# Chunked mLSTM in a fused decoder step: the chunk states move ahead of the last page sum on VectorE, and the first head runs two projection tiles further

## The chip, the cores and the metric

The kernel runs on one core of a Trainium2 chip as one program. The metric is the device time of one execution in microseconds (us). The engines named below are TensorE (PE in the profile, its weight loads PEld), VectorE (DVE), ScalarE (ACT), GpSimd (POOL) and SyncE (SP), whose queue issues most of the transfers.

## The reference

One layer of a hybrid decoder over a prompt of 512 tokens and 8 single sample tokens, all in fp32:

```python
mod = silu(c) @ w_ada + b_ada            # shift, scale, gate
h   = rms_norm(x, norm_g) * (1 + scale) + shift
z   = h @ w_in                           # att q,k,v,gate | mLSTM q,k | v | o | gate | i,f | ga | gm
ya  = (moba_attention(q, k, v) * silu(za)) @ w_att
# mLSTM: 4 heads, key width 128, value width 256
qk  = silu(causal_conv4(qk_pre));  m = running max;  w = exp(decays - m)
num = a * (C @ q) + (q @ k.T * w) @ v;   den = a * (n @ q) + rowsum(q @ k.T * w)
h_m = num / max(|den|, exp(-m));  C, n = decayed C, n plus k.T @ v
ym  = (rms_norm(h_m) * m_norm_g * sigmoid(o) * silu(zm)) @ w_mlstm
y   = rms_norm(x + gate * ((sigmoid(ga) * ya + sigmoid(gm) * ym) @ w_out))
```

For the 8 sample tokens attention reads whole pages of a cache (`cache_v`, 128 pages of 128 rows by 512 values), weighted with a softmax over the blocks that each query chose ("the page choice").

## The kernel before, in words

The program is written engine by engine, each with its own instruction list, and the lists meet in counting semaphores. Nothing is ordered by a scheduler: the order of the lines is the order of the work on each engine.

**Projection tiles.** The long product h @ w_in is cut into tiles of 128 output columns, numbered n (`T_ML` is the first of the mLSTM, 8 for each head). A tile takes 48 matmuls of 260 columns (`ztile`, L565): fp32 is split into a high and a low part, and three products are summed. Ahead of it SP loads the weights into one of four slots of `wraw` (L390), ACT rounds them to the high part (`high`, L1025), POOL subtracts to get the low part (`low`, L1521); both go into one of two slots. Behind it ACT copies the result out of PSUM (`leave`, L1030). Tile n needs tile n-2 to have left, and `high` of tile n needs tile n-2 to be done.

**One head of the mLSTM.** Tiles 0 and 1 of a head are q and k before the convolution, 2 and 3 are v, 4 and 5 the output gate, 6 and 7 the silu gate. After tiles 0 and 1 DVE convolves (`convolve`, L1911 and L1914), ACT applies silu (L1302) and computes the decays `wt` and `qd`. PE multiplies q and k (L787), turns k (L792) and v (L807) over; DVE forms `wt`, `qd` and `kw` (L2037, L2039, L2042), the weights' products. PE forms each chunk's state from `kw` (L823, "k_mm"), DVE runs them together into `Cs` (L2050, L2052) and raises `cs_rdy`; PE needs it for the outputs (L829, L831, "pv"). ACT squares these (L1321), DVE normalises (`norm`, from L2007), ACT scales (L1327), PE turns them over (L844), DVE applies the gates (L2066, L2069). PE lays tiles 4 to 7 of the head between those steps, and tiles 0 and 1 of the next head follow.

**Page values beside it.** Under each head the pages of `cache_v` are worked off in 8 steps of 4 pages: SP loads a step into one of four slots (L407), POOL multiplies it by its weights (`value_step`, L1599), and DVE sums two steps at a time (`value_pair`, L1993 and L1998). A pair's sum frees its two slots (`pair_free`), and SP waits for that before it loads the next steps; weights' tiles stand behind those loads in the same queue. PE sums over the partitions at the end of the head's last tile (`page_sums`, L580). The last pair of head h-1, `value_pair(6, h-1)`, stands in head h on DVE, between `kw` and the chunk states.

**The first head** is written apart: during it the page choice for the samples is finished on DVE (`choice_sums` L1976, `choice_total` L1980, `choice_normalise`), with a product on PE in between (L813) that waits for the sums and stands ahead of k_mm.

Of the kernel before, what the change touches and what calls it, by code (L numbers as in the profile page):

```python
# [20 lines left out]
ACT = mybir.ActivationFunctionType  # L21
# [17 lines left out]
MH, MQ, MV = 4, 128, 256  # L39
# [50 lines left out]
def decoder_step(nc, I, O):  # L90
# [14 lines left out]
    with ExitStack() as ctx:  # L105
# [443 lines left out]
        def _(pe):  # L549
# [223 lines left out]
            def mlstm(h, first, begun=False):  # L773
                n = T_ML + 8 * h
                if not first:
                    if not begun:
                        ztile(0, n, hH, hL)
                    ztile(1, n + 1, hH, hL)
                    spread_max(h)
                    ztile(2, n + 2, hH, hL)  # L780
                    ztile(3, n + 3, hH, hL)
                    pe.wait_ge(hn_ev, 2 * h + 1)
# [26 lines left out]
                if first:  # L809

                    pe.wait_ge(vt_ev, 1)
                    pe.wait_ge(sel_dve, 7)
                    mm(ps[:, 7, 256:320], ones[:, :], mxA[:, :], start=True, stop=True).then_inc(sel_pe, 1)  # L813
                else:
                    ztile(0, n + 4, hH, hL)
# [8 lines left out]
                last.then_inc(k_mm, 1)  # L824
                if not first:
                    ztile(1, n + 5, hH, hL)
# [5 lines left out]
                last.then_inc(pv_mm, 1)  # L832
                if not first:
                    ztile(2, n + 6, hH, hL)
                ztile(3, n + 7, hH, hL, pages_of=None if first else h)
                if first:
                    ztile(0, n + 8, hH, hL)
                pe.wait_ge(hn_ev, 2 * h + 3)
# [176 lines left out]
        def _(act):  # L1015
# [269 lines left out]

            def mlstm(h, first):
                n, quad = T_ML + 8 * h, T_ML // 4 + 2 * h
                if first:
                    decays(h, True)
                else:  # L1290
                    high(2, n + 2, quad)
                    act.wait_ge(z_done, n + 3)
                    last_tap(0, h)
                    leave(0, n, pre[:, 0, 3:3 + NT], ACT.Copy, chunk(preS, h))
                    high(3, n + 3, quad)
                    act.wait_ge(z_done, n + 1 + 3)
                    last_tap(1, h)
                    leave(1, n + 1, pre[:, 1, 3:3 + NT], ACT.Copy, chunk(preS, h + MH))
                    decays(h, False)
                    for e in range(2):  # L1300
                        act.wait_ge(cv_rdy, 2 * h + e + 1)
                        f(qkc[:, e, :], ps[:, 4 + e, :], ACT.Silu).then_inc(sg_rdy, 1)  # L1302
                    high(0, n + 4, quad + 1)
                    leave(0, n + 2, mvT[:, 0, :], ACT.Copy, chunk(vS, 2 * h))
                    high(1, n + 5, quad + 1)
                    leave(1, n + 3, mvT[:, 1, :], ACT.Copy, chunk(vS, 2 * h + 1))
# [4 lines left out]
                if first:  # L1311
                    high(0, n + 8, quad + 2)
                    leave(0, n + 6, gz[:, 0, :], ACT.Silu, chunk(gzS, 2 * h))
                else:
                    for u in range(2):
                        high(2 + u, n + 6 + u, quad + 1)
                        leave(u, n + 4 + u, go[:, u, :], ACT.Sigmoid, chunk(goS, 2 * h + u))
# [11 lines left out]
                if not first:  # L1329
                    high(0, n + 8, quad + 2)  # L1330
                    leave(0, n + 6, gz[:, 0, :], ACT.Silu, chunk(gzS, 2 * h))
                high(1, n + 9, quad + 2)
                if first:
                    leave(1, n + 7, gz[:, 1, :], ACT.Silu, chunk(gzS, 2 * h + 1))
                else:
                    act.wait_ge(z_done, n + 10)
# [12 lines left out]
            mlstm(0, True)  # L1349
            with act.Fori(0, MH - 1) as h:  # L1350
                mlstm(h + 1, False)
            act.dma_start(O["conv_s"][0, :, 0:2, :], I["state_conv"][0, :, 1:3, :]).then_inc(st_misc, 16)
# [154 lines left out]
        def _(pool):  # L1507
# [98 lines left out]
            for j in range(3):  # L1606
                low(j, T_ML + 4 + j)
            pool.wait_ge(w_exp, 1)
            low(3, T_ML + 7)
            causal_weights(0)  # L1610
            pool.wait_ge(sel_act, 2)
            value_step(0, 0)
            low(0, T_ML + 8)
            for s in range(1, 4):
                value_step(s, 0)
            low(1, T_ML + 9)
            low(2, T_ML + 10)
            value_step(4, 0)
            low(3, T_ML + 11)
            value_step(5, 0)  # L1620
# [73 lines left out]
        def _(dve):  # L1694
# [333 lines left out]
            def mlstm(h, first):  # L2028
# [4 lines left out]
                if not first:  # L2033
                    value_pair(4, h - 1, h == 1)
                dve.wait_ge(st_mm, h + 1)
                dve.wait_ge(w_rdy, h + 1)
# [7 lines left out]
                if first:  # L2044
                    choice_sums()
                    choice_total()
                else:
                    value_pair(6, h - 1, h == 1)
                dve.wait_ge(k_mm, h + 1)
# [7 lines left out]
                if first:  # L2057
                    choice_normalise()
                norm(h)
                value_pair(0, h, first)  # L2060
# [235 lines left out]
```

## Time and profile before

| what | us |
|---|---|
| median of 3 runs | 740.52 (737.6 to 742.81) |
| the profiled execution | 742.74 |
| its span, first to last instruction | 741.0 |
| PE busy in the span | 664.1 (90%) |
| POOL, DVE, ACT busy | 434.9, 482.4, 333.2 |
| mean granted clock of TensorE | 0.949 of full speed |

The busy times are sums over all stages. The mLSTM heads lie between about 262 and 500 us of the span: the first from 262 to 305, then three of about the same shape. Times in the rows below are us from the span's start. A matmul's own duration includes its latency, so consecutive starts tell more than durations do.

### The profile page before, as it was taken

What the parts mean: (1) busy time and instruction counts of PE and PEld (TensorE: products, weight loads), DVE (VectorE), ACT (ScalarE), POOL (GpSimd) and SP (SyncE); (2) the same over time, 40 slices, a digit from 0 to 9 for tenths busy, and PEclk for the clock granted to TensorE, in tenths of its full rate; (3) what the DMA queues carried; (4) which work ended last, traced back from release to release, by engine and by line L of the source; (5) the groups of instructions that cost most, each with busy time, mean ns of one, the idle gap of its engine ahead of it and who ended that gap; (6) DMA issues with size and microseconds to landing.
All of it is one profiled execution on the core that took longest, in us unless ns stands there. A gap on an engine that the chain in (4) does not pass through costs nothing.

```text
span 741.0 us, 14542 instructions
## 1 busy us (share of the span) xinstructions
PE 664.1 (90%) x4898; PEld 600.4 (81%) x4898; DVE 482.4 (65%) x500; ACT 333.2 (45%) x732; POOL 434.9 (59%) x290
## 2 busy tenths in 40 slices
PE   2899898797997977987999799799999999999996
PEld 0578787586877866976999699699799999999974
DVE  0627587798989953995587579565564549444435
ACT  5645838164571451642554336253322224332643
POOL 5212586474965337488589498944386567666520
PEclk9899999899999896998999899899899999999998
DMA  8968379898896883477568756756946446832302
GB/s 315 343 212 251 115 214 268 242 270 266 268 297 192 284 239 103 111 219 205 157 211 240 209 168 183 210 150 192 274 117 193 124 144 181 264 96 85 87 23 93
DMA packets 156908, 144.79 MB, mean 195 GB/s; under 512 B 7547, under 2 KB 115152, under 8 KB 156852
## 3 DMA queue, kind: packets, MB, share of 16 engines
q1 hardware_dynamic: 142984, 137.15, 62.2%
q10 hardware_dynamic: 13876, 7.02, 3.1%
q8 instruction: 27, 0.44, 0.2%
q14 instruction: 21, 0.17, 0.1%
HBM read 135.10 MB, written 9.11 MB: 195 GB/s over the span
## 4 chain that ended last, share of the span: by engine, by line
PE 37%; issue 19%; POOL 19%; DVE 10%; SPq 7%; DMA 4%; ACT 4%; POOLq 0%; ACTq 0%; DVEq 0%
PE ps L565 27%; POOL sb_wL L1521 8%; POOL sb_arenaA L1599 7%; POOL sb_arenaA L1567 4%; PE ps L995 3%; SPq L406 2%; DVE sb_arenaA L1998 2%; SPq L407 2%; DMA sb_arenaA<-in_w_ada 2%; DMA sb_wraw<-in_w_in 2%; PE ps L597 1%; DVE sb_arenaB L1998 1%; PE ps L829 1%; DVE sb_arenaA L1993 1%; PE ps L936 1%
## 5 line engine op out<-in xcount | busy, mean ns | idle before, releaser
L1521 POOL TENSOR_TENSOR sb_wL<-sb_wraw,sb_wH 128x512 fp32r<-128x512 f32 (+1 forms) x168 | 217.0, 1308 | 202.6 <-ACT sb_wH L1025 188.7
L565 PE MATMUL ps<-sb_hH,sb_wH 128*128 128x260 f32 x1152 | 242.6, 292 | 4.2 <-POOL sb_wL L1521 4.2
L565 PE MATMUL ps<-sb_hH,sb_wL 128*128 128x260 f32 x1152 | 235.9, 287 | 0.0
L565 PE MATMUL ps<-sb_hL,sb_wH 128*128 128x260 f32 x1152 | 235.8, 287 | 0.0
L565 PEld LDWEIGHTS ps<-sb_hH,sb_wH 128*128 128x128 f32 x1152 | 182.5, 193 | 18.7 <-issue 13.0
L565 PEld LDWEIGHTS ps<-sb_hL,sb_wH 128*128 128x128 f32 x1152 | 181.7, 193 | 0.0
L565 PEld LDWEIGHTS ps<-sb_hH,sb_wL 128*128 128x128 f32 x1152 | 181.7, 193 | 0.0
L1025 ACT ACTIVATE sb_wH<-sb_wraw 128x512 fp32r<-128x512 f32 (+1 forms) x168 | 98.9, 612 | 179.4 <-PE ps L565 125.7
L1599 POOL TENSOR_TENSOR sb_arenaA<-sb_arenaA 128x2048 f32<-128x2048 f32 x28 | 101.4, 3624 | 2.5 <-DMA sb_arenaA<-in_cache_v 2.5
L1567 POOL TENSOR_TENSOR sb_arenaA<-sb_arenaA 128x1024 f32<-128x1024 f32 x22 | 63.5, 2906 | 40.9 <-DMA sb_arenaA<-in_cache_k 40.9
L1852 DVE TENSOR_REDUCE sb_arenaA<-sb_arenaA 128x2048 f32 (+1 forms) x32 | 73.0, 2285 | 5.7 <-POOL sb_arenaA L1567 3.3
L1848 DVE TENSOR_TENSOR sb_arenaA<-sb_arenaA 128x2048 f32<-128x2048 f32 x21 | 54.5, 2594 | 9.4 <-DMA sb_arenaA<-in_cache_k 8.4
L1993 DVE TENSOR_REDUCE sb_arenaA<-sb_arenaA 128x512 f32<-128x4096 f32 x7 | 53.4, 7634 | 0.0
L1998 DVE TENSOR_REDUCE sb_arenaA<-sb_arenaA 128x512 f32<-128x4608 f32 x4 | 34.3, 8587 | 4.8 <-POOL sb_arenaA L1599 4.8
L1030 ACT ACTIVATE sb_arenaB<-ps 128x520 f32<-128x520 f32 (+1 forms) x57 | 33.9, 595 | 0.9 <-ACT sb_kqN L1241 0.8
L1998 DVE TENSOR_REDUCE sb_arenaB<-sb_arenaA 128x512 f32<-128x4608 f32 x3 | 25.3, 8418 | 13.8 <-POOL sb_arenaA L1599 13.8
L829 PE MATMUL ps<-sb_arenaB 128*128 128x257 f32 x32 | 16.8, 655 | 18.1 <-DVE sb_arenaB L2052 18.1
L671 PE MATMUL ps<-sb_arenaB 64*128 64x384 f32 (+3 forms) x64 | 20.9, 462 | 8.1 <-ACT sb_arenaA L1170 6.7
L829 PEld LDWEIGHTS ps<-sb_arenaB 128*128 128x128 f32 x32 | 10.0, 329 | 21.7 <-DVE sb_arenaB L2052 19.5
L1145 ACT ACTIVATE sb_arenaB<-ps,sb_nmx 128x512 f32<-128x512 f32 (+3 forms) x32 | 16.4, 526 | 22.9 <-DVE sb_nmx L1834 22.8
L1321 ACT ACTIVATE sb_arenaB<-ps 128x256 f32<-128x256 f32 x16 | 5.9, 384 | 46.0 <-PE ps L831 46.0
L597 PE MATMUL ps<-sb_arenaA,sb_gated 128*32 128x512 f32 x112 | 16.1, 691 | 10.6 <-DMA sb_arenaA<-in_w_ada 10.6
(406 smaller groups left out, 941.8 us busy)
## 6 DMA issues: line engine op xcount, KB each, us to landing
sb_wraw<-in_w_in SPq DMA_DIRECT2D x64, 512.0 KB, 5.4
sb_arenaA<-in_cache_k SPq DMA_DIRECT2D x128, 256.0 KB, 3.2
sb_arenaA<-in_cache_v SPq DMA_DIRECT2D x128, 256.0 KB, 3.2
sb_arenaA<-in_w_ada SPq DMA_DIRECT2D x6, 2048.0 KB, 12.1
sb_arenaB<-in_state_C SPq DMA_DIRECT2D x8, 512.0 KB, 4.2
sb_wraw<-in_w_mlstm SPq DMA_DIRECT2D x8, 512.0 KB, 4.5
sb_wraw<-in_w_out SPq DMA_DIRECT2D x8, 512.0 KB, 3.8
sb_arenaB<-in_x_prompt SPq DMA_DIRECT2D x1, 2048.0 KB
```

The costliest lines, as they stand in the source:

```text
L565: last = mm(ps[:, 2 * s + a, 0:HALF], w[:, s, k, :], x[:, k, a * HALF:(a + 1) * HALF], start=(k == 0 and w is wH and x is xH), stop=(k == ...
L597: last = mm(ps[32 * g:32 * g + 32, bank, :], (hS if i == W_Q else cT)[:, k, :], ada[:, i % 2, k, :], start=(k < 4), stop=(k >= 4))
L829: last = mm(ps[:, 4 + q, 0:MV + 1], wt[:, q, :], v1[:, q, :], start=True, stop=(q == 0))
L1025: f(wH[:, j % 2, part], wraw[:, j % 4, part], ACT.Copy).then_inc(hi_done, 1)
L1030: ins = f(halves(dst), zps(j % 2), func)
L1521: tt(wL[:, j % 2, part], wraw[:, j % 4, part], wH[:, j % 2, part].bitcast(F32), ALU.subtract)\
L1567: last = tt(two, two, qbc[:, s // 4:s // 4 + 1, :].broadcast_to([P, 2, AW]), ALU.mult)
L1599: tt(heads, heads, score[:, bass.ds((8 * h + s) * 32, 32)].unsqueeze(2).broadcast_to([P, 32, DH]), ALU.mult).then_inc(pool_mult, 1)
L1848: chain(tt(four, four, qbc[:, s // 4:s // 4 + 1, :].broadcast_to([P, STEP_PAGES, AW]), ALU.mult))
L1852: v.tensor_reduce(score[:, bass.ds((8 * t + s) * 32, 32)], page[:, s % 4, :].rearrange("p (g n) -> p g n", n=DH), AX, ALU.add)\
L1993: v.tensor_reduce(vhalf, vpairs[0], AX, ALU.add).then_inc(pair_free[0], 1)
L1998: v.tensor_reduce(vacc[e], vpairs[1], AX, ALU.add).then_inc(pair_free[1], 1)
```

## The change

Four engines' lists are edited; no arithmetic changes.

- DVE: for all heads but the first, `value_pair(6, h-1)` moves from ahead of the chunk states to behind them (ahead of `norm`). In the first head `choice_sums` moves from behind `kw` to ahead of `wt`.
- PE: in the first head tile 7 moves from behind pv to ahead of k_mm, tile 0 of the next head from there to between k_mm and pv, and tile 1 of the next head, so far the second head's, stands behind pv. The second head begins with `spread_max`.
- ACT: the high parts and the copies out follow that order, and the high part of the next head's tile 2 is made there too.
- POOL: in the first head the low part of tile 7 goes ahead of the wait for the decays and of the causal mask (L1593), and value steps and low parts alternate.

```diff
@@ PE, mlstm
                 if not first:
                     if not begun:
                         ztile(0, n, hH, hL)
-                    ztile(1, n + 1, hH, hL)
+                        ztile(1, n + 1, hH, hL)
                     spread_max(h)
@@
                     mm(ps[:, 7, 256:320], ones[:, :], mxA[:, :], start=True, stop=True).then_inc(sel_pe, 1)
+                    ztile(3, n + 7, hH, hL)
                 else:
                     ztile(0, n + 4, hH, hL)
@@
                 last.then_inc(k_mm, 1)
-                if not first:
+                if first:
+                    ztile(0, n + 8, hH, hL)
+                else:
                     ztile(1, n + 5, hH, hL)
@@
                 last.then_inc(pv_mm, 1)
-                if not first:
+                if first:
+                    ztile(1, n + 9, hH, hL)
+                else:
                     ztile(2, n + 6, hH, hL)
-                ztile(3, n + 7, hH, hL, pages_of=None if first else h)
-                if first:
-                    ztile(0, n + 8, hH, hL)
+                    ztile(3, n + 7, hH, hL, pages_of=h)
@@ ACT, mlstm
-            def mlstm(h, first):
+            def mlstm(h, first, begun=False):
...
-                    high(2, n + 2, quad)
+                    if not begun:
+                        high(2, n + 2, quad)
...
                     high(0, n + 8, quad + 2)
                     leave(0, n + 6, gz[:, 0, :], ACT.Silu, chunk(gzS, 2 * h))
+                    high(1, n + 9, quad + 2)
+                    leave(1, n + 7, gz[:, 1, :], ACT.Silu, chunk(gzS, 2 * h + 1))
+                    high(2, n + 10, quad + 2)
...
-                high(1, n + 9, quad + 2)
-                if first:
-                    leave(1, n + 7, gz[:, 1, :], ACT.Silu, chunk(gzS, 2 * h + 1))
-                else:
+                    high(1, n + 9, quad + 2)
...
             mlstm(0, True)
-            with act.Fori(0, MH - 1) as h:
-                mlstm(h + 1, False)
+            mlstm(1, False, True)
+            with act.Fori(0, MH - 2) as h:
+                mlstm(h + 2, False)
@@ POOL
+            low(3, T_ML + 7)
             pool.wait_ge(w_exp, 1)
-            low(3, T_ML + 7)
             causal_weights(0)
             pool.wait_ge(sel_act, 2)
-            value_step(0, 0)
-            low(0, T_ML + 8)
-            for s in range(1, 4):
+            for s in range(4):
                 value_step(s, 0)
-            low(1, T_ML + 9)
-            low(2, T_ML + 10)
+                low(s, T_ML + 8 + s)
             value_step(4, 0)
-            low(3, T_ML + 11)
             value_step(5, 0)
@@ DVE, mlstm
                     value_pair(4, h - 1, h == 1)
+                if first:
+                    choice_sums()
                 dve.wait_ge(st_mm, h + 1)
...
                 if first:
-                    choice_sums()
                     choice_total()
-                else:
-                    value_pair(6, h - 1, h == 1)
                 dve.wait_ge(k_mm, h + 1)
...
                 if first:
                     choice_normalise()
+                else:
+                    value_pair(6, h - 1, h == 1)
                 norm(h)
```

## Rows read from the trace of the kernel before

**Rows 1.** The waits, PE: who waited for whom, us in total, times, longest.

```profile
PE ps L829 <- DVE sb_arenaB L2052: 18.1, 4, 5.6
```

**Rows 2.** Timeline of PE, third head, last row fourth: start, us, what, count [idle before <- releaser].

```profile
394.83 0.49 PE L565 MATMUL ps<-sb_hH,sb_wH 128*128 128x260 f32 x2
...
400.66 1.90 PE L823 MATMUL ps<-sb_arenaB 128*128 128x257 f32 x8
...
413.56 2.08 PE L829 MATMUL ps<-sb_arenaB 128*128 128x257 f32 x4 [5.25 <-DVE sb_arenaB L2052]
...
419.22 0.59 PE L565 MATMUL ps<-sb_hH,sb_wH 128*128 128x260 f32 x2
...
478.57 2.08 PE L829 MATMUL ps<-sb_arenaB 128*128 128x257 f32 x4 [5.25 <-DVE sb_arenaB L2052]
```

**Rows 3.** Timeline of DVE, third head.

```profile
398.07 0.68 DVE L2042 SCALAR_TENSOR_TENSOR sb_arenaB<-ps,sb_wa 128x512 f32<-128x512 f32 x1
402.92 8.47 DVE L1998 TENSOR_REDUCE sb_arenaB<-sb_arenaA 128x512 f32<-128x4608 f32 x1 [4.18 <-POOL sb_arenaA L1599]
411.53 0.43 DVE L2050 COPY sb_arenaB<-ps 128x257 f32<-128x257 f32 x1
411.99 1.51 DVE L2052 SCALAR_TENSOR_TENSOR sb_arenaB<-sb_arenaB,sb_wa,ps 128x257 f32<-128x257 f32 x3
421.21 0.16 DVE L2007 TENSOR_SCALAR sb_dl<-ps 128x4 f32<-128x4 f32 x1 [7.70 <-ACT sb_arenaB L1321]
...
438.40 8.62 DVE L1998 TENSOR_REDUCE sb_arenaA<-sb_arenaA 128x512 f32<-128x4608 f32 x1 [1.61 <-POOL sb_arenaA L1599]
```

**Rows 4.** Windows: us, busy of PE, PEld, DVE, ACT, POOL, granted clock, DMA.

```profile
402.30:408.30 6.00, 6.00 (x50) 5.79 (x48) 5.38 (x1) 1.80 (x4) 6.00 (x4) 1.00 0.89 279
...
413.50:419.30 5.80, 5.74 (x15) 4.60 (x15) 0.01 (x1) 0.00 (x0) 1.51 (x1) 0.52 0.79 235
```

**Rows 5.** Timeline of SP's queue, third head.

```profile
412.21 3.83 SPq L407 DMA_DIRECT2D sb_arenaA<-in_cache_v  x4
416.32 0.38 SPq L390 DMA_DIRECT2D sb_wraw<-in_w_in  x1
```

**Rows 6.** The page, DMA issues: count, KB each, us to landing.

```profile
sb_wraw<-in_w_in SPq DMA_DIRECT2D x64, 512.0 KB, 5.4
```

**Rows 7.** Windows: one period of the third head (same columns).

```profile
380.00:444.00 64.00, 58.76 (x448) 56.57 (x447) 46.21 (x33) 29.28 (x67) 48.70 (x26) 0.95 0.67 198
```

**Rows 8.** Timeline of PE, first head and the start of the second.

```profile
272.87 1.04 PE L807 MATMUL ps<-sb_ident,sb_arenaB 128*128 128x128 f32 x8
280.51 0.66 PE L813 MATMUL ps<-sb_mxA,sb_ones 128*128 128x64 f32 x2 [6.60 <-DVE sb_mxA L1976]
...
286.77 2.08 PE L829 MATMUL ps<-sb_arenaB 128*128 128x257 f32 x4 [2.07 <-DVE sb_arenaB L2052]
...
292.57 0.69 PE L565 MATMUL ps<-sb_hH,sb_wH 128*128 128x260 f32 x2
...
328.55 1.07 PE L807 MATMUL ps<-sb_ident,sb_arenaB 128*128 128x128 f32 x8 [2.76 <-ACT sb_vS L1032]
```

**Rows 9.** Timeline of DVE, first head to the second head's convolution.

```profile
274.57 3.29 DVE L2039 TENSOR_TENSOR sb_arenaB<-sb_arenaB 128x384 f32<-128x384 f32 x1
...
278.38 1.98 DVE L1976 TENSOR_REDUCE sb_mxA<-sb_arenaA 128x64 f32<-128x1024 f32 x1
...
294.74 0.16 DVE L2007 TENSOR_SCALAR sb_dl<-ps 128x4 f32<-128x4 f32 x1 [7.29 <-ACT sb_arenaB L1321]
...
305.83 1.42 DVE L2066 SCALAR_TENSOR_TENSOR ps<-ps,sb_vcol,sb_arenaB 128x512 f32<-128x512 f32 x2 [1.29 <-PE ps L844]
...
317.21 0.82 DVE L1911 TENSOR_SCALAR ps<-sb_arenaB,sb_vcol 128x512 f32<-128x512 f32 x1 [0.22 <-DVE sb_arenaA L1998]
```

**Rows 10.** Timeline of ACT: end of the page choice's weights, second head's last silu.

```profile
271.44 0.29 ACT L1268 ACTIVATE sb_selfp<-sb_selfp 128x64 f32<-128x64 f32 x1
...
323.53 0.60 ACT L1302 ACTIVATE sb_arenaB<-ps 128x512 f32<-128x512 f32 x1 [2.49 <-DVE ps L1914]
```

## The prediction

> **What bounds the kernel now.** I read the table of busy times first: PE is busy 664.1 of 741.0 us, more than any other engine, so what is to be had without taking work from PE is its idle time, and the time in which its clock is low. The waits of PE come next. They show the idle time as few, large pieces: 18.1 us in four waits of pv (L829) for the last instruction of the chunk states on VectorE (L2052), one in each head [rows 1], and 6.60 us in one wait of the page choice's product (L813) for `choice_sums` [rows 8]. Both lie where the change is made.
>
> The timeline of the third head tells what such a wait costs. The tile behind k_mm starts at about 402.2 and takes as long as the one ahead of it, 400.66 - 394.83 = 5.83 us; so PE is done with it near 408.1. pv starts only at 413.56, and lasts to 419.22, 5.66 us [rows 2]. In that stretch the granted clock is 0.52 of full speed, so the lower level of 1.2 GHz, where it was 1.00 (2.4 GHz) in the tile before the idle time [rows 4]. PE's idle time therefore costs twice: 5.25 us, and about half of the 5.66 us after it, 2.83 us. A second way gives the same: k_mm's four products take 402.2 - 400.66 = 1.56 us at full clock, 0.39 us each, so pv's seven would take 2.7 instead of 5.66, 2.9 us saved.
>
> Why is VectorE late? It has `kw` at 398.75 and k_mm is over at 402.2, but it first waits 4.18 us for GpSimd's last value step and then sums the pair, 402.92 to 411.4. The states take 411.53 to 413.5, 2.0 us [rows 3]. So 9 us of the queue stand between the states and their inputs, none of them needed by the states.
>
> **The third and fourth head.** The states now start at 402.3 and end at 404.3, while PE is in its tile until 408.1: the cover is 3.8 us. pv runs 408.1 to 410.9 at full clock. ScalarE's squares follow, and `norm` started 421.21 - 419.22 = 2.0 us behind pv's end [rows 2, 3]; that makes 412.9. VectorE's moved pair now runs from 404.4 (GpSimd's step was ready at 402.9) to 412.9 with its 8.47 us. The two meet, so the pair is just hidden; I allow 0.2 us for it. What follows hangs on pv and `norm`: scaling, the high and low part of the next head's tile 0, tiles 6 and 7. All moves up by 5.25 + 2.83 - 0.2 = 7.9 us.
>
> Does anything behind keep it from staying? I laid one period out again with PE's work back to back. Its length was 478.57 - 413.56 = 65.0 us, from one head's pv to the next's [rows 2], and becomes 57.1, which is PE's own work at full clock. GpSimd is busy 48.70 us in 64 and VectorE 46.21 [rows 7]; both fit in 57, each with some 8 us of slack. SyncE is the closest. The moved pair frees page slots 2 and 3 and ended 0.8 us before the page loads at 412.21; they took 3.83 us to issue, and the weights of the next head's tile 1 stood behind them, at 416.32 [rows 5]. Now the pair ends at 412.9, so these weights are issued near 417.8 and land 5.4 us later [rows 6], 423.2. PE comes to that tile at 431.6 (pv's end 410.9, two tiles 11.7, page sums and turning over some 2.9, one tile 5.8, in all 431.3), and both parts of it need about 4 us: a margin of 4 us. The page loads are later against PE by 1.5 + 8 us only for this one pair; GpSimd takes them when it has the low part of tile 0 done, some 0.6 us later than otherwise. The convolution starts when the pair of steps 2 and 3 is summed, and the start of that sum kept its distance to PE in my layout within 0.2 us. So each of these two heads gives 7.9 us.
>
> **The states beside GpSimd.** `L2052` now runs while GpSimd multiplies or subtracts. Its three instructions took 1.51 us at 411.99, when GpSimd was busy as well. `qd` (L2039), which reads two tensors of SBUF, took 3.29 us in the first head [rows 9], where a value step ran. Were each of the three states to take that in place of its 0.5 us, they would take 3 x 2.8 = 8.4 us more and end at 412.7, and PE would idle 4.6 us again. The Trainium skill (GPSIMD Engine Reference, the table of the engine's SBUF interfaces) says that GpSimd contends with VectorE instructions that have two SBUF inputs or run in a two-port mode. The states read one tensor from SBUF and one from PSUM, so by that rule they are free of it, and 1.51 us agrees; I take no cost.
>
> **The first head.** PE turned v over until 273.9, then idled 6.60 us and did the page choice's product at 280.51, k_mm, and pv from 286.77 to 292.57 with 2.07 us of idle time in between; pv's 5.8 us are again the slow ones [rows 8]. The weights that `choice_sums` needs are there at 271.7 [rows 10]. Moved ahead, it runs 271.8 to 273.8, the product follows at 274.1 or so, and tile 7 at 274.7. `wt`, `qd` and `kw` end near 278.4 even if `qd` takes its 3.29 us again, hidden by the tile, which ends at 280.6. Were that cover gone, PE would wait 3.7 us. k_mm to 282.2, tile 8 to 288.1 with the states under it (284.5), pv to 291.1, tile 9 to 297. The ends of the queues of ACT and POOL hold: the high parts of tiles 7, 8 and 9 are wanted 2 us or more after they can be made; ScalarE waits for tile 8's end at 288.1 to make half of tile 10, and is free when pv ends at 291.1.
>
> So pv ends 1.5 us earlier, and PE has tile 9 behind it, which it did not have before. But the second head's start is set by VectorE, not by PE: `norm` 294.74 becomes 293.2; the first pair's sum, the gates (whose 1.29 us of waiting for PE falls away, since the turning over comes after tile 9 at 298.3) and the second pair's sum follow back to back, and the convolution starts at 314.4 in place of 317.21 [rows 9]: 2.8 us. Its last silu was at 323.53 [rows 10] and comes at 320.8. PE, which has tiles 10 and 11 left, finishes them near 312.1 (about 1.5 us of it a new wait for ScalarE, which copies the state out and issues two stores before it empties tile 8). Then it idles until 321.4, **9.3 us**: the time that the earlier tiles won is held here, and is no gain by itself.
>
> Such an idle time lowers the clock. What was slow after 5.25 us of it was the next 5.7 us [rows 2, 4]. v's turning over waits here for its copy, as it did for 2.76 us before [rows 8], now until 325.8; behind it tile 12 runs, slow for its first half: 2.9 us. It ends near 335.4, where it ended 335.2 before: no gain by then. From there the second head is as the third: k_mm, a tile to 342.9, no wait for the states (VectorE has them at 339), pv to 345.8, where it was 354.2. The first two heads give **8.3 us**, with 11.2 if the clock is up by tile 12, and 5.5 if k_mm is slow as well.
>
> **The sum.** 8.3 + 2 x 7.9 = 24.1 us. The stage behind the heads starts from the fourth head's last pair of sums and page loads, which keep their distance; nothing there is changed. 742.74 - 24.1 = 718.6 for the profiled execution. That one is 2.2 us above the median of the three runs; from the median it is 716.4. I say 717.
>
> **Rivals.**
> *(a) The order's next limit bites.* The layout has VectorE, SyncE's page loads and GpSimd each with a few us to spare, and durations of transfers vary more than that when 8 us less are there for the same bytes (DMA share 0.67 in the period [rows 7], it would be 0.76). For it: the pair sum's end and `norm` meet exactly, and ScalarE's wait for weights. If each of three heads keeps 3 us of idle time and with it no full fall of the clock, the gain is 24.1 - 9 = 15 us: 727.5 from the profiled time, 725.5 from the median.
> *(b) The clock does not fall at the second head, and smaller waits close up:* 24.1 + 2.9 + 1 = 28: 712.5 from the median. Against it: 9.3 us are more than any idle time that left it up.
> *(c) It is the page loads' turn: slower.* The moved pair frees slots 2 and 3 later, and the weights stand behind those loads. Place: SyncE's queue at tile 9 of each head. It decides from the point where the pair ends more than 4 us later than my 412.9. It begins to cost more than the change brings at 12 us, which needs GpSimd's last step (ready at 402.9, VectorE at 404.4) some 13 us late. Then each of three heads would lose its 7.9 and 3 to 5 us more with a low clock behind: about +12 us, 752. Nothing in the profile points to it: that step never waited for its pages.
> *(d) The states' move does nothing,* because pv waits for something else too. pv waits for `cs_rdy` alone behind k_mm, and L2052 ends 0.1 us before pv starts [rows 2, 3]. If it were so, only the first head's 2 to 3 us would be left: 738.
>
> **Chances.** Forecast 62%, (a) 20%, (b) 10%, (c) 3%, (d) 5%. The forecast's own range is 713 to 721 (one head's 2.9 us of clock either way, and 1 us of the runs' spread). The range takes in (b)'s 712.5 and the nearer half of (a): 712 to 727. A measurement of this kernel tells a change of about 1%, 7.4 us, from none. Faster by over 1%: forecast, (a) and (b), with a little taken off: 0.91. Within 1%: 0.05. Slower: 0.04.
>
> **What would show it.** Right: the idle time in front of L829 gone in all heads, the granted clock 1.00 during pv, L2052 ahead of the L1998 that writes to arenaB, a period of 57 us, the idle time at L813 gone and a new one of about 9 us in front of the second head's L787, with a low clock after it. Wrong: idle time in front of a tile's first matmul, released by GpSimd's L1521, in heads 3 and 4 (then (a) or (c)), or `norm` starting over 1 us behind the squares; and a second head that starts earlier than 320, or later.

## The result, and the profile after

| | before | after |
|---|---|---|
| median of the runs, us | 739.06 (734.34 to 742.81) | 710.21 (707.32 to 720.91) |
| the profiled execution / its span | 742.74 / 741.0 | 707.32 / 705.6 |
| PE busy | 664.1 (90%) | 648.2 (92%) |
| mean granted clock | 0.949 | 0.974 |

The ratio is 0.960, with an interval of 0.952 to 0.968. One execution of the changed kernel, the one of 720.91 us, was in a slower state, and the ratio is formed without it. I had said 717, with 712 to 727 as the range; the time lies 1.8 us below the range. Two later measurements of the same kernel gave 0.972 and 0.964; the three are weighed below.

PE's busy time fell by 16 us though it runs the same 4898 matmuls: that is the clock, not the work (the mean granted clock rose from 0.949 to 0.974). The page and PE's waits after (who waited for whom, us in total, times, longest):

```profile
PE 648.2 (92%) x4898; PEld 588.7 (83%) x4898; DVE 485.6 (69%) x500; ACT 331.8 (47%) x731; POOL 434.5 (62%) x290
```

```profile
PE ps L597 <- DMA sb_arenaA<-in_w_ada: 10.4, 3, 8.2
PE ps L787 <- issue: 9.3, 1, 9.3
...
PE ps L565 <- POOL sb_wL L1526: 3.1, 1, 3.1
...
PE ps L807 <- ACT sb_vS L1035: 1.6, 2, 1.0
```

Pv's waits for the states, 18.1 us in [rows 1], are gone from the list, and so is the 6.6 us wait of the choice's product for VectorE. A new line stands there: L787, the second head's first product, 9.3 us. "Issue" means that the profile names no releaser. The code has three waits in front of it: for the first head's scaled outputs, for its gates, and for the silu behind the convolution. The first two were over long before (the gates' last instruction on VectorE ended at 302.1); the last silu on ScalarE ended at 317.56, and L787 starts at 317.66:

```profile
316.96 0.60 ACT L1306 ACTIVATE sb_arenaB<-ps 128x512 f32<-128x512 f32 x1 [2.50 <-DVE ps L1915]
```

PE's timeline after, second and third head, beside [rows 2, 8] (L824, L832 and L834 are the old L823, L829 and L831):

```profile
317.66 2.04 PE L787 MATMUL ps<-sb_arenaB 128*128 128x128 f32 x8 [9.27 <-issue]
319.50 1.06 PE L792 MATMUL ps<-sb_ident,sb_arenaB 128*128 128x128 f32 x4
321.58 1.06 PE L807 MATMUL ps<-sb_ident,sb_arenaB 128*128 128x128 f32 x8 [1.02 <-ACT sb_vS L1035]
322.40 0.49 PE L565 MATMUL ps<-sb_hH,sb_wH 128*128 128x260 f32 x2
...
335.70 1.03 PE L832 MATMUL ps<-sb_arenaB 128*128 128x257 f32 x4
...
338.55 0.59 PE L565 MATMUL ps<-sb_hH,sb_wH 128*128 128x260 f32 x2
...
393.05 1.03 PE L832 MATMUL ps<-sb_arenaB 128*128 128x257 f32 x4
...
449.81 1.03 PE L832 MATMUL ps<-sb_arenaB 128*128 128x257 f32 x4
```

Pv now follows its tile at once and takes 338.55 - 335.70 = 2.85 us in place of 5.66. From pv of the second head to pv of the fourth it is 449.81 - 335.70 = 114.1 us, two periods of 57.35 and 56.76 us.

VectorE's timeline after, second head, beside [rows 3]. The states come first, then the pair (L1999), then `norm`:

```profile
325.23 0.70 DVE L2045 SCALAR_TENSOR_TENSOR sb_arenaB<-ps,sb_wa 128x512 f32<-128x512 f32 x1
330.18 0.43 DVE L2050 COPY sb_arenaB<-ps 128x257 f32<-128x257 f32 x1 [4.24 <-PE ps L824]
330.64 1.52 DVE L2052 SCALAR_TENSOR_TENSOR sb_arenaB<-sb_arenaB,sb_wa,ps 128x257 f32<-128x257 f32 x3
332.08 8.50 DVE L1999 TENSOR_REDUCE sb_arenaB<-sb_arenaA 128x512 f32<-128x4608 f32 x1
340.73 0.16 DVE L2008 TENSOR_SCALAR sb_dl<-ps 128x4 f32<-128x4 f32 x1
```

Windows after (us, busy of PE, PEld, DVE, ACT, POOL, granted clock, DMA): the second head's first products, its tile 4 (tile 12 of the count), and one period of the later heads, beside [rows 4, 7]:

```profile
317.60:320.10 2.50, 2.44 (x11) 2.47 (x12) 2.50 (x1) 1.93 (x5) 1.94 (x2) 0.50 1.07 349
322.40:328.30 5.90, 5.90 (x52) 5.90 (x51) 3.54 (x4) 1.57 (x3) 5.90 (x4) 1.00 0.57 158
...
335.70:392.70 57.00, 56.45 (x454) 55.19 (x453) 46.88 (x33) 29.20 (x67) 50.17 (x26) 1.00 0.76 226
```

In the period PE is busy 56.45 of 57.0 us at a clock of 1.00; it bounds the later heads completely. GpSimd has 6.8 us left, VectorE 10. In the first head PE's idle time has shrunk to 0.25 us in front of the choice's product and 0.99 us in front of a later tile, and the second head's convolution starts at 310.65. VectorE's timeline there:

```profile
299.46 1.39 DVE L2068 SCALAR_TENSOR_TENSOR ps<-ps,sb_vcol,sb_arenaB 128x512 f32<-128x512 f32 x2
300.89 1.23 DVE L2071 TENSOR_TENSOR sb_gated<-ps,sb_arenaB 128x1024 f32<-128x1024 f32 x1
302.03 8.40 DVE L1999 TENSOR_REDUCE sb_arenaA<-sb_arenaA 128x512 f32<-128x4608 f32 x1
310.65 0.81 DVE L1912 TENSOR_SCALAR ps<-sb_arenaB,sb_vcol 128x512 f32<-128x512 f32 x1 [0.22 <-DVE sb_arenaA L1999]
```

**Where the 35.4 us of span went.** I laid both traces beside one another at five points on PE: an earlier product of the page choice, L799, in front of which nothing is changed, L787 of the second head, pv of the second head and of the fourth, and the samples' first product (L936, after L939). The last column is what my sum has for the same stretch; differences are taken before rounding.

| stretch | before | after | less | my sum |
|---|---|---|---|---|
| start to L799 (unchanged code) | 265.8 | 263.0 | 2.7 | 0 |
| to the second head's L787 | 58.5 | 54.6 | 3.8 | 2.8 |
| to its pv | 24.2 | 18.0 | 6.2 | 2.7 |
| to the fourth head's pv | 130.1 | 114.1 | 16.0 | 15.8 |
| to the samples' product | 53.0 | 49.4 | 3.6 | 2.8 |
| to the end (unchanged code) | 209.4 | 206.4 | 3.1 | 0 |

A stretch ends where pv starts, so the clock that pv itself gains counts in the line behind it: 2.8 us of each pv, the fourth's in the fifth line. So 29.6 us lie in the heads, where I had 24.1, and 5.8 us in stretches that the change doesn't touch. The largest difference from my sum, 3.5 us, stands in the third line, from the second head's L787 to its pv.

### The profile page after: what moved, and what is told of

The parts are those of the page before. It is cut to its first block, busy times and chain, and to the rows that moved or that the text cites. A ratio compares the mean times of both kernels' runs of the same rounds, so it can differ in the third digit from the quotient of the medians.

```text
span 705.6 us, 14507 instructions
## 1 busy us (share of the span) xinstructions
PE 648.2 (92%) x4898; PEld 588.7 (83%) x4898; DVE 485.6 (69%) x500; ACT 331.8 (47%) x731; POOL 434.5 (62%) x290
## 4 chain that ended last, share of the span: by engine, by line
PE 53%; DVE 14%; issue 10%; SPq 9%; ACT 5%; DMA 4%; POOL 4%; ACTq 0%; DVEq 0%; POOLq 0%
PE ps L565 39%; SPq L406 5%; SPq L407 4%; DVE sb_arenaA L1999 4%; PE ps L998 3%; DVE sb_arenaA L1849 2%; DMA sb_wraw<-in_w_in 2%; POOL sb_wL L1526 2%; POOL sb_arenaA L1604 1%; DVE sb_arenaB L1999 1%; DMA sb_arenaB<-in_x_sample 1%; DVE sb_arenaA L1853 1%; PE ps L824 1%; ACT sb_wH L1028 1%; DMA sb_arenaA<-in_cache_k 1%
## 5 line engine op out<-in xcount | busy, mean ns | idle before, releaser
L565 PEld LDWEIGHTS ps<-sb_hH,sb_wH 128*128 128x128 f32 x1152 | 180.6, 192 | 19.3 <-issue 12.5
L565 PEld LDWEIGHTS ps<-sb_hH,sb_wL 128*128 128x128 f32 x1152 | 179.7, 191 | 0.0
L1572 POOL TENSOR_TENSOR sb_arenaA<-sb_arenaA 128x1024 f32<-128x1024 f32 x22 | 61.2, 2807 | 37.3 <-DMA sb_arenaA<-in_cache_k 37.3
L1999 DVE TENSOR_REDUCE sb_arenaA<-sb_arenaA 128x512 f32<-128x4608 f32 x4 | 34.2, 8552 | 5.5 <-POOL sb_arenaA L1604 5.5
L2195 DVE TENSOR_TENSOR sb_arenaB<-ps,sb_arenaB 128x520 f32 x8 | 5.6, 700 | 30.1 <-PE ps L565 30.1
L1999 DVE TENSOR_REDUCE sb_arenaB<-sb_arenaA 128x512 f32<-128x4608 f32 x3 | 25.5, 8504 | 0.0
L597 PE MATMUL ps<-sb_arenaA,sb_gated 128*32 128x512 f32 x112 | 15.4, 671 | 10.7 <-DMA sb_arenaA<-in_w_ada 10.4
L2129 DVE CAST sb_kqr<-sb_rowsel 40x128 fp32r (+1 forms) x8 | 6.8, 855 | 20.3 <-PE ps L939 19.9
L671 PEld LDWEIGHTS ps<-sb_arenaB 64*128 64x128 f32 x64 | 10.0, 190 | 13.0 <-ACT sb_arenaA L1173 5.3
```

The lines of the kernel that those rows point to most:

```text
L565: last = mm(ps[:, 2 * s + a, 0:HALF], w[:, s, k, :], x[:, k, a * HALF:(a + 1) * HALF], start=(k == 0 and w is wH and x is xH), stop=(k == ...
L671: last = mm(ps[:, b, c:c + (q + 1) * P], qT[r, q * P:(q + 1) * P], kT[r, 0:(q + 1) * P], start=True, stop=True)
L1572: last = tt(two, two, qbc[:, s // 4:s // 4 + 1, :].broadcast_to([P, 2, AW]), ALU.mult)
L1999: v.tensor_reduce(vacc[e], vpairs[1], AX, ALU.add).then_inc(pair_free[1], 1)
```

## The experiments

**The two parts alone.** First the pair's move by itself, on the kernel before:

```diff
@@ DVE, mlstm, kernel before
-                else:
-                    value_pair(6, h - 1, h == 1)
                 dve.wait_ge(k_mm, h + 1)
...
                     choice_normalise()
+                else:
+                    value_pair(6, h - 1, h == 1)
```

> The kernel before with one edit: value_pair(6, h-1) behind the chunk states on VectorE. Theory 1 (a wait for the states costs its idle time and the slow clock after it): three waits of 5.3 to 5.6 us and 2.8 us of clock behind each go, 3 x 8 = 24 us less than before; the first head keeps its 6.6 and 2.1 us of idle time; period 57 us. Rival (the heads are only free because the first head runs ahead): the second head keeps a wait and the gain is 16 us or less.

715.12 us, ratio 0.972 (0.966 to 0.978), 23 us less. Pv to pv over two periods took 114.0 us. In its waits L829 is left with the first head's alone:

```profile
PE ps L813 <- DVE sb_mxA L1976: 6.6, 1, 6.6
...
PE ps L829 <- DVE sb_arenaB L2050: 2.1, 1, 2.1
```

So all three waits go without the first head's part, and the rival falls. Then the reverse, the changed kernel with the pair put back:

> The changed kernel with value_pair(6, h-1) put back ahead of the states. Theory 1: the second head's convolution starts some 3 to 4 us earlier than before and nothing else is won: 4 us less than before, with the idle time in front of L787 near 9 us and three waits of pv of 5 to 6 us. Together with the pair alone it makes the whole change's 29. Rival (the long idle time lowers the clock for a tile): 1 us less than before. Rival (the two parts need one another): both alone give much less than 29 in sum.

735.54 us, ratio 0.997 (0.993 to 1.001). Its waits:

```profile
PE ps L832 <- DVE sb_arenaB L2054: 14.6, 3, 5.3
...
PE ps L787 <- issue: 9.2, 1, 9.2
```

The three waits are back (4.2, 5.0 and 5.3 us), and the first head's part alone is worth 0.3%, 2.7 us where I expected 4, which is no more than the interval. Measured beside one another, the pair's move alone and the whole change took 715.12 and 715.36. Later both were measured again, with more executions:

> The kernel before with the pair's move alone, again, beside the whole change on the same chip. From the first page product of the choice to pv of the second head it took 77.3 us where the whole change took 72.7 and 75.1: so 2 to 4 us more than the whole change. If the first head's part is worth nothing, the two are equal within 1 us.

714.20, ratio 0.967 (0.964 to 0.971), against 711.55, 0.964 (0.961 to 0.968), for the whole change: 2.7 us more, but the intervals overlap.

**Which part of the first head's edit counts.** VectorE's two moves with the tiles, high and low parts where they were:

```diff
@@ DVE, mlstm, kernel before, with the pair's move as above
+                if first:
+                    choice_sums()
                 dve.wait_ge(st_mm, h + 1)
...
-                    choice_sums()
                     choice_total()
```

> The kernel before with VectorE's two moves alone (choice_sums ahead of wt, value_pair(6) behind the states); the tiles of the first head stand as before. Theory 1: the product for the choice no longer waits 6.6 us, k_mm starts 2 to 4 us earlier, and since the second head's start hangs on VectorE, which gains the same there as with the tiles moved, the stretch from the choice's product to the second head's pv takes 73 to 75 us as in the changed kernel: the tiles' new order is worth nothing by itself. Rival (the tiles' order matters): 76 to 77 us, as with the pair alone, and 2 us more in all than the changed kernel.

711.90, ratio 0.965 (0.962 to 0.969). From L799 to the second head's pv it took 337.55 - 263.64 = 73.9 us, where the changed kernel took 72.7, 75.1 and 74.3 in its three profiles, and the pair alone 77.3 and 76.3. PE's timeline in its first head:

```profile
275.12 0.43 PE L813 MATMUL ps<-sb_mxA,sb_ones 128*128 128x64 f32 x2 [0.25 <-ACT sb_arenaB L1309]
277.00 2.82 PE L823 MATMUL ps<-sb_arenaB 128*128 128x257 f32 x8 [1.45 <-DVE sb_arenaB L2044]
281.90 2.08 PE L829 MATMUL ps<-sb_arenaB 128*128 128x257 f32 x4 [2.07 <-DVE sb_arenaB L2051]
```

PE idles here in small pieces, and is there for the second head all the same: it waits 0.62 us in front of L787, where the changed kernel waits 9.27. The two numbers agree with the changed kernel's: the tiles' new order, which is most of the diff, is worth nothing that I can measure. It mostly moves PE's idle time from the first head to in front of L787.

**The changed kernel again.**

> The changed kernel again, for a second profile. If the clock behind the second head's idle time was up early by the way the kernel works, L787 to the next k_mm takes 10.6 us again and the span lies within 2 us of 705.6. If it is chance, tile 12 takes 5.8 us in some executions and up to 8.7 in others, and the span moves by up to 3 us at each such place. Against before: 29 us less.

715.36, ratio 0.972 (0.968 to 0.976); span 714.2. L787 to k_mm took 10.9 us, but L799 came at 266.8, 3.8 us later than in the first profile, in unchanged code. A third measurement:

> The changed kernel a third time, for what it is worth on average: its median was 29 us under the kernel before in one session and 23 us in the next. If my sum of 24 is right and the rest was chance, 22 to 28 us less than before, ratio 0.963 to 0.970. If the first session's 29 is the kernel's, 0.960 or less.

711.55, ratio 0.964 (0.961 to 0.968). The three ratios, 0.960, 0.972 and 0.964, make 29.6, 20.7 and 26.6 us of 740. And the kernel before:

> The kernel before, for a second profile. What lies in front of the first changed instruction took 263.0 us and 266.8 us in two profiles of the changed kernel, so it moves by 4 us by itself. Three waits of 5.3 us in front of L829 and a granted clock of 0.52 behind each again, if they follow from the order of the work.

733.77, a single execution; L799 at 262.0, waits of 5.28 and 5.27 us in front of pv in the third and fourth head, but 3.6 in the second, and 4.08 in front of the choice's product instead of 6.60. In the second head the clock was low in tile 12 this time (L787 to k_mm 13.1 us, against 11.0 in [rows 8]'s profile), and that hid 2 us of pv's wait: what the clock took from PE there, VectorE had been making PE wait for anyway.

From L799 to the samples' product the kernel before took 265.8 and 262.2 us in its two profiles, the changed one 236.2, 239.5 and 237.9. The means differ by **26.1 us**. That is my best number for the change, cleared of the unchanged parts; it rests on two and three profiles, which differ among themselves by up to 3.6 and 3.3 us.

**Where the pair may stand.** The changed kernel with the pair one step later:

```diff
@@ DVE, mlstm, changed kernel
                     choice_normalise()
-                else:
-                    value_pair(6, h - 1, h == 1)
                 norm(h)
+                if not first:
+                    value_pair(6, h - 1, h == 1)
```

> The changed kernel with value_pair(6, h-1) behind norm: the pair ends some 11 us later against PE, so its page slots, and the weights behind their loads in SyncE's queue, come 11 us later. By my prediction's margin of 4 us, PE waits for tile 1 of the next head, or for the page sums and the convolution, 4 to 6 us in each of three heads, and with some slow clock: 12 to 20 us more than the changed kernel, some 725 to 730. If the margin were over 11 us, nothing would change (710).

748.24, ratio 1.014 (1.008 to 1.020): 1.4% slower than the kernel before, and 32.9 us more than the changed one measured beside it, where I expected 12 to 20. Timelines of the second head's end, VectorE, SyncE's queue, GpSimd, ScalarE and PE:

```profile
346.67 8.52 DVE L1999 TENSOR_REDUCE sb_arenaB<-sb_arenaA 128x512 f32<-128x4608 f32 x1
```

```profile
356.01 3.83 SPq L407 DMA_DIRECT2D sb_arenaA<-in_cache_v  x4
360.12 0.38 SPq L390 DMA_DIRECT2D sb_wraw<-in_w_in  x1
```

```profile
363.21 3.62 POOL L1604 TENSOR_TENSOR sb_arenaA<-sb_arenaA 128x2048 f32<-128x2048 f32 x1 [11.71 <-DMA sb_arenaA<-in_cache_v]
366.79 2.52 POOL L1526 TENSOR_TENSOR sb_wL<-sb_wraw,sb_wH 128x512 fp32r<-128x512 f32 x2
```

```profile
364.50 1.15 ACT L1028 ACTIVATE sb_wH<-sb_wraw 128x512 fp32r<-128x512 f32 x2 [13.13 <-DMA sb_wraw<-in_w_in]
```

```profile
368.11 0.51 PE L565 MATMUL ps<-sb_hH,sb_wH 128*128 128x260 f32 x2 [3.85 <-POOL sb_wL L1526]
...
393.73 1.97 PE L807 MATMUL ps<-sb_ident,sb_arenaB 128*128 128x128 f32 x8 [3.41 <-ACT sb_vS L1035]
```

The pair ends at 355.2, 15.5 us behind pv's start at 339.7; in the changed kernel that distance is 4.9 (340.6 and 335.7). So it ends 10.6 us later against PE, as I expected. Its slots' pages are issued at 356.0, and GpSimd waits 11.7 us for them. The weights of the next head's tile 1 stand behind those loads, at 360.1, and ScalarE waits 13.1 us for them. The low part of that tile comes after both, and PE waits 3.85 us for it. Later weights are late too: in front of the third head's L807 PE waits 3.41 us (0.56 in the changed kernel), and over the kernel ScalarE's waits for weights grew from 41.0 to 94.3 us. This is the mechanism of my rival (c), at the place that I gave. The changed kernel escapes it because its pair ends in time. There the same low part starts at 352.24:

```profile
352.24 2.54 POOL L1526 TENSOR_TENSOR sb_wL<-sb_wraw,sb_wH 128x512 fp32r<-128x512 f32 x2
```

Half of it is done at 353.5, which is all that PE waited for above, and PE comes to this tile near 359.0. That is a reserve of some 5.5 us, an estimate from these rows, where the prediction had 4. No run has the pair between the two places, so where the loss begins isn't shown.

**The long idle time and the clock.** PE busy in it:

```diff
@@ PE, mlstm, changed kernel
                     pe.wait_ge(hn_ev, 2 * h + 1)
+                    if begun:
+                        for _ in range(36):
+                            mm(ps[:, 6, 0:P], ident[:, :], ident[:, :], start=True, stop=True)
```

> The changed kernel, with 36 products of the identity with itself (into an unused bank) in the second head's idle time of 9.3 us, so that PE is busy in it; their result is thrown away. Theory 2 (the low clock behind that idle time costs what L787 and L792 show, 2.04 against 1.06 us): 1 to 1.5 us less than the changed kernel. Rival (as predicted: half a tile more, at least in most executions): 3 to 4 us less.

713.69, ratio 0.965 (0.959 to 0.971), within the changed kernel's own three, 0.960 to 0.972. Windows over L787 and L792, and over v's turning and tile 12, beside those of the changed kernel above:

```profile
320.80:322.80 2.00, 1.59 (x12) 1.36 (x12) 2.00 (x1) 1.63 (x5) 1.37 (x2) 1.00 1.08 346
324.90:333.10 8.20, 8.19 (x56) 8.20 (x57) 4.24 (x4) 1.83 (x3) 8.20 (x4) 0.79 0.63 189
```

L787 is fast now, but after the next wait, 2.42 us for v, tile 12 is slow in part. In the changed kernel it was fast in all three profiles, behind 9.3 us of idle time. From L787 to pv the filled kernel took 19.8 us, the changed one 18.0, 18.4 and 18.0. Both theories miss in this stretch: filling won nothing there, and the clock was low in another place. The total can't tell a gain of 1 us from none.

## A version that beats both

The second head's start hangs on VectorE. In the first head of the changed kernel the product of `choice_normalise` takes 3.38 us of its queue, and the engine then idles 4.58 us ahead of `norm`:

```profile
281.91 3.38 DVE L1986 TENSOR_TENSOR sb_selfp<-sb_selfp,sb_mxA 128x64 f32<-128x64 f32 x1
289.87 0.16 DVE L2008 TENSOR_SCALAR sb_dl<-ps 128x4 f32<-128x4 f32 x1 [4.58 <-ACT sb_arenaB L1328]
```

A pair's sum of 7.5 us fits into those 8 us, if the normalising is put off:

```diff
@@ DVE, mlstm, changed kernel
+                if h == 1:
+                    choice_normalise()
                 dve.wait_ge(k_mm, h + 1)
...
                 if first:
-                    choice_normalise()
+                    value_pair(0, h, first)
                 else:
                     value_pair(6, h - 1, h == 1)
                 norm(h)
-                value_pair(0, h, first)
+                value_pair(2 if first else 0, h, first)
...                                           (behind the gates)
-                value_pair(2, h, first)
+                if not first:
+                    value_pair(2, h, first)
```

> The changed kernel, in the first head value_pair(0) ahead of norm and value_pair(2) ahead of the gates, and choice_normalise put off to the second head. Theory 3 (the second head's start hangs on VectorE's queue alone, of which 4.6 us are idle ahead of norm, 3.4 us choice_normalise held up): the convolution starts 7 us earlier, the idle time in front of L787 falls from 9.3 to about 2 us, and the kernel takes 7 to 8 us less than the changed one, about 702. Rival (page loads or GpSimd set it): 0 to 3 us less, with a new wait for L1526 or the page loads.

704.73, ratio 0.953 (0.946 to 0.959), 9 us under the filled kernel measured beside it. VectorE's timeline in the first head:

```profile
283.04 7.56 DVE L1994 TENSOR_REDUCE sb_arenaA<-sb_arenaA 128x512 f32<-128x4096 f32 x1
293.67 8.45 DVE L1999 TENSOR_REDUCE sb_arenaA<-sb_arenaA 128x512 f32<-128x4608 f32 x1
302.33 1.42 DVE L2070 SCALAR_TENSOR_TENSOR ps<-ps,sb_vcol,sb_arenaB 128x512 f32<-128x512 f32 x2 [0.21 <-DVE sb_arenaA L1999]
303.78 1.23 DVE L2073 TENSOR_TENSOR sb_gated<-ps,sb_arenaB 128x1024 f32<-128x1024 f32 x1
305.11 0.81 DVE L1912 TENSOR_SCALAR ps<-sb_arenaB,sb_vcol 128x512 f32<-128x512 f32 x1
```

The convolution starts at 305.1, against L799 5.7 us earlier than in the changed kernel, where I expected 7, and PE idles 2.07 us in front of L787. Again, with more executions:

> The kernel with the first head's sums earlier, again, for its ratio with five rounds: 0.953 of the kernel before, 7 us under the changed kernel; the stretch from the choice's product to the second head's pv 66 to 69 us.

705.99, ratio 0.957 (0.954 to 0.960); L799 to pv 67.1 us. And with both remaining idle times of the second head filled:

> The kernel with the first head's sums earlier, and in the second head 8 products of the identity ahead of the wait for silu and 7 ahead of the wait for v (into banks not in use; results thrown away), which fill idle times of 2.1 and 1.6 us. In the kernel without them the stretch from L787 to pv took 19.7 us with a clock of 0.83, and 18.0 in the changed kernel. Theory 2b (short idle times let the clock fall there): the stretch takes 16.5 to 17 us, and the kernel 2 to 3 us less than without filling. Rival (the clock's fall is not tied to these idle times): 19 to 20 us again, no gain.

704.66, ratio 0.955 (0.952 to 0.959), 6.9 us under the changed kernel measured beside it, with intervals that don't meet. L787 to pv took 17.4 us at a clock of 1.00, against 19.6 (0.83) and 17.6 (0.90) without filling. The clock was up, but the total doesn't show it: at most 2 us, inside the intervals.

All three runs have the tiles in their new order. Whether VectorE's earlier sums would win as much with the old order was not tested. With VectorE's moves alone PE was only 0.62 us early at the second head's L787, so there it had little to gain from a silu that comes sooner; the tiles' order, worth nothing by itself, may be what this version needs.

## Why the prediction was wrong, point by point

- **The wait for the states, and its price** (5.25 us, 2.83 us of clock, 0.2 us off: 7.9 a head). Right. Two periods of 65.1 on average became two of 57.05; the pair met `norm` as laid out (ended 340.6, `norm` at 340.73); pv took 2.85 us where I had 2.8.
- **The states beside GpSimd.** Right: 1.52 us. `qd` took 1.44 us, not 3.29; it was hidden either way. The product of `choice_normalise`, which reads two tensors of SBUF, took 3.38 us in the new order, with a value step on GpSimd from 281.6 to 285.2, and 0.23 us in the kernel before. The sum has no term for it; it was hidden in front of `norm`.
- **The first head, and the 9.3 us in front of L787.** Right: 9.27 us. That VectorE sets the second head's start is shown by the version that frees VectorE (idle time down to 2.07), and by VectorE's moves alone, which do as well as the whole change. The convolution came 3.8 us earlier against L799, not 2.8: `norm` started 2.1 us earlier where I had 1.5, and 0.4 us more fell away behind it. PE also ran out of tiles 1 us sooner than I had it, so that the 9.3 us came out right with both of its ends off by the same 1 us, which is luck.
- **The step that failed: "behind it tile 12 runs, slow for its first half: 2.9 us".** In the changed kernel's three profiles the clock was up by tile 12, and L787 to k_mm took 10.6, 10.9 and 10.6 us where I had 14.0. I took one observation (5.7 us slow after 5.25 us idle) for a rule. That is the term of the sum that was mis-sized: it cost about 3 us less than I charged. From L799 to the end of the second head's pv the gain was 12.9 us in the first pair of profiles, and 10.6 us by the means of the two and the three, where I had 8.3. The prediction had this case as its 11.2 "if the clock is up by tile 12". Its rival (b), with 10%, said that the clock does not fall at all; it did fall (L787 took 2.04 us, at 0.50) and came back sooner than I thought. I called the idle time right and the clock behind it wrong.
- **The range.** Its lower end was 712, half a us under rival (b), and it took no account of how far one measurement lies from another. The changed kernel's medians were 710.2, 715.4 and 711.6, and in one profile against another up to 3.8 us lay in code that is the same. The first profile is 11.3 us under my 718.6 for it: 5.8 us of that lie in unchanged code, 3.5 in the stretch with the failed term, 1.0 in front of it and 1.0 behind it. So with the failed term right the forecast would still have been above 712, near 714. My 24.1 us stands against 26.1 by the profiles' stages, and against 20.7 to 29.6 by the three ratios. What the first measurement had beyond the others goes with the granted clock as far as the profiles tell: the changed kernel's three spans of 705.6, 714.2 and 707.4 us had mean clocks of 0.974, 0.958 and 0.976, and up to L799 0.95, 0.93 and 0.96. Why the clock was granted more in one than in another stays open; no run tells it.
- **Rival (c)** had the right mechanism and place, and its margin of 4 us was near the 5.5 that the changed kernel's rows give. Its price was near too: I had some 12 us over the kernel before if the pair came 12 us late, and 10.6 us of delay cost 10 us over that kernel (748.24 against 738.26). The 12 to 20 us that I then expected of the experiment, over the changed kernel, were too low. **(a)** and **(d)** did not come.

## What to carry to other kernels

Ask of each step in an engine's queue whether the step behind it needs it: two moves on VectorE won all of the 3.5%, and the large reordering of tiles around them won nothing measurable by itself, since another engine's queue set the time at which they were wanted. A step that also frees buffers has a latest place as well as an earliest; one step further, and the same sum made the kernel slower than before. Price the slow clock behind an idle time from several traces, as something that happens or not, and take the spread from one measurement of the same kernel to the next into the range.

## What the runs showed of the hardware that I had not expected

The fall of TensorE's clock is not told by the length of the idle time in front. In the second head, from L787 to k_mm (10.0 us at full clock):

| idle before L787, before L807 | us from L787 to k_mm |
|---|---|
| 9.27, 1.02 / 9.22, 1.32 / 9.26, 1.00 (changed) | 10.6 / 10.9 / 10.6 |
| 9.22, 1.26 (pair behind norm) | 10.8 |
| 9.22, 0.98 (first head's part alone) | 12.4 |
| 0.61, 2.76 / 0.42, 3.49 (before) | 11.0 / 13.1 |
| 0.63, 3.14 / 0.58, 2.32 (pair alone) | 12.9 / 10.5 |
| 0.62, 2.46 (VectorE's moves alone) | 12.2 |
| 1.27, 2.42 (filled) | 12.3 |
| 2.07, 1.57 / 2.07, 0.60 (sums earlier) | 12.2 / 10.1 |

Five profiles have the 9.2 to 9.3 us in front of nearly the same stretch; four took 10.6 to 10.9 us and one 12.4. The granted clock shows what differed. Windows over the idle time, over L787 and L792, and behind them, in the changed kernel and then with the first head's part alone:

```profile
308.40:317.60 9.20, 0.00 (x0) 0.00 (x0) 8.77 (x10) 1.23 (x3) 5.84 (x2) 0.62 0.82 248
317.70:321.50 3.80, 2.86 (x12) 2.45 (x12) 3.80 (x1) 3.17 (x8) 3.34 (x4) 0.58 1.01 319
321.60:328.20 6.60, 6.60 (x56) 6.60 (x57) 4.34 (x4) 1.72 (x3) 6.60 (x4) 1.00 0.61 169
```

```profile
309.20:318.30 9.10, 0.00 (x0) 0.00 (x0) 8.67 (x10) 1.20 (x3) 5.56 (x2) 0.69 0.90 248
318.40:322.20 3.80, 2.89 (x12) 2.49 (x12) 3.80 (x1) 3.20 (x8) 3.31 (x4) 0.50 0.98 316
...
324.00:327.30 3.30, 3.30 (x20) 3.30 (x20) 2.60 (x4) 0.61 (x1) 3.30 (x3) 0.64 0.45 127
```

In both the clock had fallen while PE was still idle (0.62 and 0.69 over the idle time), so that part of the slow time cost nothing. In the first it was up again by 321.6, 4 us after PE resumed; in the second it was still low in part after 324.0, 5.6 us after. How much of the low clock falls into the idle time and how much on work is what a long idle time leaves open.

In the stage behind the heads, idle times in front of the samples' first product were followed by a pair of tiles at full clock in three profiles (idle 0.74, 1.06 and 1.27 us; 12.3 us from one such product to the next). In the others the pair took 13.8 to 13.9 us, after idle times of 0.37 to 2.16 us or none, and 15.1 and 15.4 us after 0.93 and 1.60. What did hold: in every profile without a wait in front of pv the granted clock was 1.00 through the third and fourth head, but for the late pair, which has other waits there; and behind each wait of over 5 us in front of pv it was low.
